# Splitting a weight panel in two halves, with a semaphore count for each

## The reference

```python
def first_block(...):            # stick-breaking attention, SwiGLU, a gated side input
    hn = rms_norm(h, norm_mix[i])
    h = h + stick_breaking_attention(hn, sb_w_in[j], sb_w_out[j])   # 16 heads of 64
    h = h + swiglu(rms_norm(h, norm_ffn[i]), ffn_w_in[i], ffn_w_out[i])   # D_FF 2816
    gate = sigmoid(rms_norm(h, norm_ple[i]) @ ple_w_gate[i])
    h = h + gate * (p[i] @ ple_w_proj[i])
# second_block: a gated convolution over 31 tokens beside a retention with 4 heads of 256,
#               then a layer norm and pointwise weights ("pw")
# third_block:  an S5 branch and an SSD branch (16 heads) from one wide projection, a GLU, a gated side input
```

## Time and profile before

| what | value |
|---|---|
| median of 3 runs | 3895.08 us (3892.99 to 3896.93) |
| span of the profiled execution, first to last instruction | 3891.3 us |
| mean granted clock of TensorE | 0.975 |
| TensorE busy | 3673.2 us, 94% |
| VectorE busy | 2153.1 us, 55% |
| GpSimd busy | 961.0 us, 25% |
| ScalarE busy | 940.7 us, 24% |

### The profile page before, as it was taken

How to read it: one execution, slowest core, us unless ns; L and a number is a source line. 1 busy time by engine, 2 the same in 40 slices (tenths; PEclk the granted TensorE clock), 3 DMA queues, 4 the chain that set the end, 5 groups by cost and what they waited for, 6 DMA issues and landing times.

```text
span 3891.3 us, 45707 instructions
## 1 busy us (share of the span) xinstructions
PE 3673.2 (94%) x18230; PEld 2917.4 (75%) x18230; DVE 2153.1 (55%) x2828; ACT 940.7 (24%) x1672; POOL 961.0 (25%) x541
## 2 busy tenths in 40 slices
PE   6999999899999999999999999879999999999998
PEld 5677676688888877788876677558778877787776
DVE  5455546633334347799923452464715498663565
ACT  3434345300000003211101101140222112552132
POOL 2121211232333323233321121123222232014322
PEclk9999999999999999899999999989999999999999
DMA  2000100121212121122211121211174323532111
GB/s 94 17 28 22 33 23 23 54 66 60 70 59 65 59 65 44 39 97 81 86 65 55 38 76 49 77 64 60 60 152 109 78 83 114 150 98 81 66 49 65
DMA packets 139236, 260.16 MB, mean 67 GB/s; under 512 B 45632, under 2 KB 87616, under 8 KB 136000
## 3 DMA queue, kind: packets, MB, share of 16 engines
q1 hardware_dynamic: 72208, 156.26, 13.9%
q10 hardware_dynamic: 66864, 101.62, 7.6%
HBM read 209.35 MB, written 46.14 MB: 66 GB/s over the span
## 4 chain that ended last, share of the span: by engine, by line
PE 85%; DVE 9%; ACT 1%; issue 1%; DMA 1%; SPq 1%; POOL 1%; ACTq 0%; DVEq 0%; POOLq 0%
PE bank L596 24%; PE bank L598 23%; PE bank L597 23%; PE bank L827 2%; PE bank L1004 2%; PE bank L864 1%; DVE fb L2128 1%; PE bank L847 1%; PE bank L993 1%; PE bank L714 1%; DVE ab L2131 1%; PE bank L1165 1%; PE bank L1148 1%; DVE h L2520 1%; DVE scan L2519 1%
## 5 line engine op out<-in xcount | busy, mean ns | idle before, releaser
L596 PE MATMUL bank<-xh,wh 128*128 128x512 f32 x3024 | 1195.5, 395 | 45.1 <-POOL wl L565 20.2
L597 PE MATMUL bank<-xl,wh 128*128 128x512 f32 x3024 | 1185.0, 392 | 0.0
L598 PE MATMUL bank<-xh,wl 128*128 128x512 f32 x3024 | 1184.4, 392 | 0.0
L563 POOL CAST wh<-raw 128x1024 fp32r<-128x1024 f32 x264 | 283.1, 1073 | 2746.5 <-PE bank L598 2695.6
L596 PEld LDWEIGHTS bank<-xh,wh 128*128 128x128 f32 x3024 | 570.8, 189 | 187.4 <-issue 27.4
L565 POOL TENSOR_TENSOR wl<-raw,wh 128x1024 fp32r<-128x1024 f32 x264 | 662.6, 2510 | 21.1
L598 PEld LDWEIGHTS bank<-xh,wl 128*128 128x128 f32 x3024 | 570.7, 189 | 123.1 <-issue 0.8
L597 PEld LDWEIGHTS bank<-xl,wh 128*128 128x128 f32 x3024 | 571.3, 189 | 119.0 <-issue 1.0
L2297 DVE SCALAR_TENSOR_TENSOR bank<-apad,cols,bank 128x512 f32<-128x512 f32 x406 | 267.9, 748 | 0.0
L2033 DVE TENSOR_TENSOR h<-bank,h 128x512 f32<-128x512 f32 x240 | 165.4, 691 | 163.8 <-PE bank L598 163.7
L2128 DVE TENSOR_TENSOR_SCAN fb<-fb 128x256 f32<-128x256 f32 (+7 forms) x128 | 189.5, 1521 | 74.6 <-ACT ab L1370 74.6
(11 more groups left out here) (333 smaller groups left out, 5091.3 us busy)
## 6 DMA issues: line engine op xcount, KB each, us to landing
raw<-in_wstream SPq DMA_DIRECT2D x264, 512.0 KB, 3.5
spills<-spill ACTq DMA_DIRECT2D x38, 512.0 KB, 2.8
rawm<-in_mod_w ACTq DMA_DIRECT2D x12, 1024.0 KB, 4.9
gate_spill<-gates ACTq DMA_DIRECT2D x16, 512.0 KB, 2.6
tabs<-in_rope ACTq DMA_DIRECT2D x4, 2048.0 KB, 8.1
f<-spills SPq DMA_DIRECT2D x8, 1024.0 KB, 5.9
h<-in_x ACTq DMA_DIRECT2D x4, 1024.0 KB, 12.0
tabs<-gate_spill ACTq DMA_DIRECT2D x4, 1024.0 KB, 7.5
```

Source lines behind the costliest of these rows:

```text
L563: nc.gpsimd.tensor_copy(wh[:, slot], raw[:, slot]).then_inc(S("panel_high"), 1)
L596: nc.tensor.matmul(o, lh, rh, start=start, stop=False)
L597: nc.tensor.matmul(o, lh, rl, start=False, stop=False)
L598: return nc.tensor.matmul(o, ll, rh, start=False, stop=stop)
```

## The change

The cast and the subtraction each work on four slabs, twice for a panel, and each subtraction raises `panel_split`, which so counts half panels. `split_done` gets the number of the half. TensorE waits for half 0 ahead of the first slab and for half 1 ahead of slab 4, in place of one wait for the whole panel ahead of the first. SyncE's waits are turned into the same count and still ask for the whole panel. In the two places where `split_done(..., 1)` stands alone (`dt`, `ssd_out`) TensorE waits for the whole panel as before.

```diff
+SLABS = KT // 2
+    def double(self, more=0):
+        return 2 * self.b + more if self.i is None else self.i * (2 * self.c) + (2 * self.b + more)
...
-                sp.wait_ge(S("panel_split"), q - 1)
+                sp.wait_ge(S("panel_split"), 2 * (q - 1))
...
-                nc.gpsimd.tensor_copy(wh[:, slot], raw[:, slot]).then_inc(S("panel_high"), 1)
-                pool.wait_ge(S("panel_high"), panel.value(1))
-                nc.gpsimd.tensor_tensor(wl[:, slot], raw[:, slot], wh[:, slot].bitcast(F32),
-                                        ALU.subtract).then_inc(S("panel_split"), 1)
+                for part in range(2):
+                    k = slice(part * SLABS, (part + 1) * SLABS)
+                    nc.gpsimd.tensor_copy(wh[:, slot, k], raw[:, slot, k]).then_inc(S("panel_high"), 1)
+                    pool.wait_ge(S("panel_high"), panel.double(part + 1))
+                    nc.gpsimd.tensor_tensor(wl[:, slot, k], raw[:, slot, k], wh[:, slot, k].bitcast(F32),
+                                            ALU.subtract).then_inc(S("panel_split"), 1)
...
-            def split_done(panel):
-                pe.wait_ge(S("panel_split"), panel.value(1))
+            def split_done(panel, part):
+                pe.wait_ge(S("panel_split"), panel.double(part + 1))
...
             def tile(unit, slot, slabs, rhs, between=None, split=None, panel=None):
...
                     for n, (slab, (rh, rl)) in enumerate(zip(slabs, rhs)):
+                        if panel is not None and th == 0 and slab % SLABS == 0:
+                            split_done(panel, slab // SLABS)
...
             def first_pair(unit, panel, norm):
-                split_done(panel + 1)
...
+                            if th == 0 and k % SLABS == 0:
+                                split_done(panel + m, k // SLABS)
...
-                    if n % 4 == 0:
-                        split_done(panel + n // 4)
+                    if n % 2 == 0:
+                        split_done(panel + n // 4, n % 4 // 2)
...
                 elif kind == "v":
-                    split_done(panel + 1)
...
+                            if q == 0 and k % SLABS == 0:
+                                split_done(panel + 1, k // SLABS)
...
-                split_done(panels("dt") + 1)
+                split_done(panels("dt") + 1, 1)
```

More of the change, by code:

```diff
@@ L497, in stream @@
                     for s in range(2):
-                        sp.wait_ge(S("panel_split"), i * 2 + s - 1)
+                        sp.wait_ge(S("panel_split"), i * 4 + (2 * s - 2))
                         sp.dma_start(raw[:, s].rearrange("p k n -> p (k n)"), wstream[i * 2 + s]).then_inc(
@@ L603, in bank_free, with tile @@
                     pe.wait_ge(S(f"bank_free{unit.b % 2}"), unit.half())
-            def split_done(panel):
-                pe.wait_ge(S("panel_split"), panel.value(1))
-            def tile(unit, slot, slabs, rhs, between=None, split=None):
+            def split_done(panel, part):
+                pe.wait_ge(S("panel_split"), panel.double(part + 1))
+            def tile(unit, slot, slabs, rhs, between=None, split=None, panel=None):
                 for th in range(2):
@@ L622, in tile_x @@
             def tile_x(unit, panel, high=xh, low=xl, between=None, split=None):
-                split_done(panel)
-                tile(unit, panel.b % 2, range(KT), [(high[:, k, :], low[:, k, :]) for k in range(KT)], between, split)
+                tile(unit, panel.b % 2, range(KT), [(high[:, k, :], low[:, k, :]) for k in range(KT)], between, split,
+                     panel)
             def first_pair(unit, panel, norm):
-                split_done(panel + 1)
                 slots = [(panel.b + m) % 2 for m in range(2)]
@@ L788, in attn_project @@
                     for k in range(KT):
+                        if k % SLABS == 0:
+                            split_done(panel, k // SLABS)
                         mm = mm3(banks[u][:, :], wh[:, panel.b % 2, k, :], wl[:, panel.b % 2, k, :], xh[:, k, t],
@@ L803, in attn_project @@
                     last_pair = 2 * i + 1 if kind == "out" else i
-                    split_done(panel + (n // 4 if kind == "out" else 0))
+                    if kind == "out":
+                        split_done(panel + n // 4, n % 4 // 2)
+                    else:
+                        split_done(panel, n // SLABS)
                     pe.wait_ge(S("ol_ready"), 2 * last_pair + 2)
@@ L921, in side_product @@
                 for m in range(KT):
-                    if m % 4 == 0:
-                        split_done(panels(name) + m // 4)
+                    if m % 2 == 0:
+                        split_done(panels(name) + m // 4, m % 4 // 2)
                     if m == 2:
@@ L1236, in _ @@
                         ssd_direct(c + 1)
-                split_done(panels("ssd_out") + 1)
+                split_done(panels("ssd_out") + 1, 1)
                 pe.wait_ge(S("ssd_low"), CHUNKS // 2)
```

## The result

| kernel | median of 4 runs | lowest to highest |
|---|---|---|
| before | 3896.01 us | 3892.99 to 3903.53 |
| changed | 3849.36 us | 3846.70 to 3852.60 |

The medians differ by 47 us, where the prediction said 23.5. The ratio of the two kernels is 0.9884, with a 95% interval of 0.9872 to 0.9895; by it the gain is 45 us.

A forecast was written before the change was run, and what follows sets the result against it. TensorE bounds the kernel (85% of the chain), so gains come only where it stands still. Stalls 16.9, clock 4.6 and VectorE 2 make 23.5 us less: 3895.1 to 3871.6 us, 8-in-10 range 3863 to 3884.

The forecast's parts named there:

- The price of a half: GpSimd's cast 0.57 us, subtraction 1.25 and about 0.08 between: a half in 1.9 us, a panel in 3.8.
- The sum of the stalls: TensorE's idle time waiting for GpSimd's split, over five kinds of place, shrinks by 16.9 us.
- kind 1: Four stalls behind a first pair (ffn, conv, pw, s5_u), each 1.6 us shorter: 6.4 us.
- kind 2: Five retention stalls, at the first `v`, `qk` and three `out` products, each 1.6 us shorter: 8.0 us.
- kind 3: Attention's first `v` product, waiting for two panels split one after the other: 1.2 us less.
- kind 4: Four late panels of `xbc_first` behind the gathers of `u`; only the last one counts: 1.6 us.
- The `v` product at slab 4: Half-wide matmuls finish the first half's work early, leaving 0.5 us of waiting ahead of slab 4.
- a sign that the prediction had named: New idle time of TensorE ahead of slab 4 would make the forecast wrong.
- The added waits: TensorE's 295 more waits for `panel_split`, now inside an accumulation, were taken to cost nothing.
- The clock: TensorE's granted clock partly recovers behind the five retention stalls: 4.6 us, within 0 to 9.2.
- VectorE beside GpSimd: VectorE's waits for GpSimd instructions end sooner in four places, at most 1.1 us each; 2 us taken.
- The upper rival (3863): All of it comes: clock up in all five, VectorE's waits 4 us less, a half 1.75 us; chance 0.14.

The follow-up runs named there:

- experiment 4: The kernel before, plus a second, already met wait for the whole panel where the change waits for the second half: 3895.8 us, ratio 1.0002.
- Experiment 1: The changed kernel with GpSimd still working in halves, but TensorE waiting for the whole panel as before: 3884.63 us against 3894.63, ratio 0.9974.
- experiment 7: The kernel before with only the subtraction cut in halves, cast in one piece, whole-panel waits: 3906.37 us, ratio 1.0023.

## Why the prediction came out 22 us short

- **The price of a half, 1.9 us, and of a panel, 3.8.** Right: 1.98 and 3.88.
- **The sum of the stalls, 16.9 us.** Right but for small sizes. By matched matmuls kind 1 gave 6.1 of 6.4 us, kind 2 7.4 of 8.0, kind 3 1.0 of 1.2, `dt` lost 0.4 where 0.3 was taken: 14.1 where 15.3 was taken. That is 0.1 us at each stall, since a half takes 1.98 us and not 1.9. The table's 15.1 holds 0.1 of kind 4 beside them, and 0.8 from small stalls that were not forecast.
- **The `v` product at slab 4, 0.5 us of waiting.** Right in kind, 0.3 us at most: from 1953.84 on the matmuls of slabs 0 to 3 start 0.12 us apart, and the first one of slab 4 starts 0.45 us after the one ahead of it.
- **Kind 4, 1.6 us.** Right in total, 1.4 us. The stretch from the end of TensorE's work ahead of the four panels to the start of the last one's was 2889.32, less 4.10 idle ahead of it, to 2925.78 = 40.56 us, and is 2853.91, less 2.80, to 2890.30 = 39.19, 1.4 less. This is the 1.6 us of the prediction: the last panel is used 2.10 us after its cast began, not 3.83. Idle time is only 0.3 us less, 5.94 and 5.66; the rest is matmuls that follow each other faster, which the table above counts as clock. One new stall is in it, a sign that the prediction had named: TensorE waits 0.68 us ahead of slab 4 of the first of these panels (at 2857.59). VectorE works on `spill` there, an operation with two inputs in SBUF, and the second cast and subtraction take 1.61 and 2.13 us, not 0.61 and 1.29.
- **The added waits, nothing.** Right, by experiment 4: 1.0002 [0.9993, 1.0011], within 0.016 us a wait.
- **The clock, 4.6 us of 0 to 9.2.** Too low as a whole: 9.2 (10.8 with the places of `at`) and 11.2 in two profiles, though such a sum scatters by some 3 us. The term was drawn up for the five stalls of retention alone, and there it was nearly right: 5.4 and 5.5 us, three of five kept the clock. Of the rest 1.4 is kind 4, which the prediction had under the stalls. Another 1.3 to 1.7 us each comes behind waits on VectorE and ScalarE that it did not look at: the first one for `pt` and two of glu, in both profiles. Behind the one for `pt` the granted clock of the next 5 us is 1.00, where it was 0.66. So these places count twice, in idle time and in clock.
- **VectorE beside GpSimd, 2 us. This is the step that failed.** Mechanism and rule were there, and for the four places taken 2 us was too little but inside its bounds (3.7 of at most 4.4). That the sum lies inside is luck in part: the first place gave 2.45 us, over twice the 1.1 taken as the most for one. What was wrong was the number of places. The trace was searched for stalls of TensorE on GpSimd in every panel, and for stalls on VectorE only where one was long and GpSimd stood beside it in attention. That a stall may end on VectorE or ScalarE, with GpSimd behind it at second hand, was left out for glu, for retention's `pt` and for the one near 2742. They brought 10.8 us. Experiment 1 shows that these do come from the shorter instructions alone (10 us, with dearer panels against it), and experiment 7 that at `pt` they need the short cast between two subtractions, and in glu they do not.
- **The upper rival (3863)** had the same hole: its 4 us for VectorE were again four places. So no case of the prediction could reach 3849, and the range was too narrow on that side.

The term of VectorE was mis-sized by 12.9 us in the first profile and 10.9 in the second (14.9 and 12.9 in place of 2). The clock adds 6.2 and 6.6 more, and the stalls fall short by 1.8. That is 17 and 15 of the 22 us; the rest is the distance between the profiled executions and the medians.

## What to carry to other kernels

Where two engines shut each other out, the length of an instruction on the idle one is a cost on the busy one: look for VectorE rows of one form whose time is several times its usual (2.74 us and 2.79 where the same work takes 0.68), in the whole trace, and follow who waits behind them, at second hand too. Cut the blocking work, and where the busy engine has two such operations in a row, see that a short piece stands between two long ones. Give the consumer a count for each piece; waits that are met cost nothing that these runs could tell. Keep whole the pieces whose consumer wants all of them at once.

## What the runs showed of the hardware

- In these traces GpSimd's casts and subtractions and VectorE's operations with two inputs in SBUF take turns instruction by instruction, and both pay (`vt` 1.67 us, the cast behind it 1.07). With two equal halves of a subtraction in a row, both of two VectorE operations wait (1.73 and 1.74 us) and nothing is won; a single one wins (1.66 us, not 2.74).
- GpSimd's casts and subtractions have a part of about 0.18 us that does not go with the columns: casts of 1024, 512 and 256 columns take 1.042, 0.610 and 0.397 us, subtractions 2.398, 1.292 and 0.738.
- The same idle time of 2.19 to 2.23 us in the changed kernel was followed by a full clock three times and by a lower one twice (1.00 and 0.66 granted over the next 5 us).
